# Shared-key attention with split scores: queries and keys in high and low halves, three products in place of one

## The reference, cut to what matters

```python
def dilated_group(q, k, v, slopes, window, dilation):
    ...
    scores = jnp.einsum("bpnqhd,bpnkhd->bpnhqk", qb, kw) * (1.0 / math.sqrt(dh))
    ...
    scores = jnp.where(valid[:, None], scores + bias, NEG_INF)
    m = jnp.max(scores, axis=-1, keepdims=True)
    p = jnp.exp(scores - m)
    denom = jnp.sum(p, axis=-1, keepdims=True)
    ...
def dilated_attention(x, k, v, w_q, w_o):
    q = (x @ w_q).reshape(bsz, s, N_GROUPS, N_HEADS, HEAD_DIM).astype(jnp.float32)
    for g, (window, dilation) in enumerate(DILATION_PAIRS):
        o, l = dilated_group(q[:, :, g], k, v, slopes, window, dilation)
    ...
    return out.reshape(bsz, s, N_HEADS * HEAD_DIM).astype(x.dtype) @ w_o
```

## Time and profile before

| what | value |
|---|---|
| median of 3 runs | 1755.33 us |
| profiled execution | 1756.47 us, its span 1754.7 us |
| PE busy | 1717.1 us, 98% of the span |
| DVE busy | 1243.8 us, 71% |
| ACT busy | 976.3 us, 56% |
| chain that ended last | PE 88%, DVE 7%, ACT 3%, issue 2% |
| scores of this stage, L780 | 1% of the chain |
| granted PE clock, mean | 0.992 |

### The profile page before, as it was taken

The page is one execution under the profiler, slowest core; times in us unless marked ns, Lnnn a source line. Parts: engine busy times, 40 slices in busy tenths (PEclk is TensorE's granted clock), DMA queues, the critical chain, the costliest instruction groups (busy, mean ns, idle before and its releaser), DMA issues.

```text
span 1754.7 us, 33254 instructions
## 1 busy us (share of the span) xinstructions
PE 1717.1 (98%) x11724; PEld 1559.4 (89%) x11724; DVE 1243.8 (71%) x2166; ACT 976.3 (56%) x1710; POOL 49.3 (3%) x33
## 2 busy tenths in 40 slices
PE   9999998999999999999899999999999999999998
PEld 7888898888899888888788888989999999888887
DVE  6776789777664776677787766868656567787765
ACT  5564596655455655466565544565533346665543
POOL 0000100100010000000010001001000010010000
PEclk9999999999999999999999999999999999999999
DMA  6555455455544556433255564333455533345562
GB/s 225 191 200 194 133 181 182 143 185 199 196 140 157 202 185 219 160 118 123 87 208 192 191 201 147 99 119 133 144 171 193 178 126 134 112 141 195 189 201 90
DMA packets 76349, 288.80 MB, mean 165 GB/s; under 512 B 9312, under 2 KB 11616, under 8 KB 76256
## 3 DMA queue, kind: packets, MB, share of 16 engines
q1 hardware_dynamic: 76256, 287.53, 48.6%
HBM read 286.45 MB, written 1.05 MB: 164 GB/s over the span
## 4 chain that ended last, share of the span: by engine, by line
PE 88%; DVE 7%; ACT 3%; issue 2%; DMA 0%; ACTq 0%; SPq 0%; DVEq 0%
PE psum L532 32%; PE psum L533 17%; PE psum L524 11%; PE psum L526 10%; PE psum L525 10%; DVE wlo L1580 1%; ACT whi L1105 1%; PE psum L780 1%; DVE sums L1710 1%; PE psum L610 1%; PE psum L657 1%; PE psum L662 1%; DVE r_sq L1717 1%; DVE sums L1725 1%; PE psum L696 1%
## 5 line engine op out<-in xcount | busy, mean ns | idle before, releaser
L1580 DVE TENSOR_TENSOR wlo<-raw,whi 128x1024 fp32r<-128x1024 f32 (+2 forms) x485 | 630.5, 1307 | 288.2 <-ACT whi L1105 287.4
L532 PE MATMUL psum<-x_split,whi 128*128 128x512 f32 x1760 | 618.3, 395 | 3.1 <-DVE x_split L1615 2.0
L1105 ACT ACTIVATE whi<-raw 128x1024 fp32r<-128x1024 f32 (+2 forms) x494 | 545.5, 1116 | 39.5 <-PE psum L526 20.9
L533 PE MATMUL psum<-x_split,wlo 128*128 128x256 f32 x1760 | 494.3, 281 | 0.0
L532 PEld LDWEIGHTS psum<-x_split,whi 128*128 128x128 f32 x1760 | 331.1, 188 | 80.8 <-DVE x_split L1615 2.3
L524 PE MATMUL psum<-x_split,whi 128*128 128x272 f32 (+1 forms) x1168 | 341.4, 292 | 4.5 <-DVE x_split L1780 4.2
L526 PE MATMUL psum<-x_split,wlo 128*128 128x272 f32 (+1 forms) x1168 | 333.7, 286 | 0.0
L525 PE MATMUL psum<-x_split,whi 128*128 128x272 f32 (+1 forms) x1168 | 332.8, 285 | 0.0
L533 PEld LDWEIGHTS psum<-x_split,wlo 128*128 128x128 f32 x1760 | 331.5, 188 | 0.0
L532 PE MATMUL psum<-h_split,whi 128*128 128x512 f32 x770 | 272.2, 397 | 0.0
L524 PEld LDWEIGHTS psum<-x_split,whi 128*128 128x128 f32 x1168 | 219.9, 188 | 11.4 <-issue 8.6
(11 more groups left out here) (233 smaller groups left out, 1711.0 us busy)
## 6 DMA issues: line engine op xcount, KB each, us to landing
raw<-w_in SPq DMA_DIRECT2D x264, 512.0 KB, 3.2
raw<-w_out SPq DMA_DIRECT2D x96, 704.0 KB, 4.3
raw<-w_mix SPq DMA_DIRECT2D x42, 512.0 KB, 3.3
raw<-w_rg SPq DMA_DIRECT2D x25, 512.0 KB, 3.9
raw<-w_q SPq DMA_DIRECT2D x24, 512.0 KB, 3.3
raw<-w_kv SPq DMA_DIRECT2D x16, 512.0 KB, 3.3
raw<-w_mixo SPq DMA_DIRECT2D x16, 512.0 KB, 3.2
raw<-w_rg_out SPq DMA_DIRECT2D x8, 640.0 KB, 3.9
```

Source lines behind the costliest of these rows:

```text
L532: nc.tensor.matmul(ps[:, bank, :], whi[slot][:, w], split, start=start, stop=False)
L533: return nc.tensor.matmul(part(bank, 0), wlo[slot][:, w], split[:, 0], start=False, stop=stop)
L1105: nc.scalar.activation(whi[slot][:, 0:cols], raw[slot][:, 0:cols], ACT.Copy).then_inc(w_hi_done, count)
L1580: V.tensor_tensor(wlo[slot][:, 0:cols], raw[slot][:, 0:cols], f(whi[slot][:, 0:cols]), ALU.subtract).then_inc(w_lo_done, 1)
```

## The change

Queries and keys are split too. ACT's copy of a query tile out of PSUM now writes `q_hi` in fp32r (24 times, as before); a new instruction of DVE, `rest_of_query(s)`, reads the same bank again, scales it and subtracts `q_hi`, which gives `q_lo`; it, not ACT, now signals `acc_free`. For each of the 8 pairs ACT makes `k_hi` from `kT` (`high_keys`), and DVE `k_lo` (`rest_of_keys`). `scores` issues three fp32r products in place of one float32 product, for each of two query halves and two heads, and waits also for `k_lo_done`. DVE's `rest_of_query(s)` stands at the end of step s, behind `bias_max`, `sum_groups` and `rest_of_output`; the keys of pair hp are split in step max(0, 3 hp - 2).

```diff
--- before.py
+++ after.py
@@ -205,7 +205,7 @@
     cursor[0] = mix_at
     kT = place("kT", [KD, SEQ])
     v_tok = place("v_tok", [2, D])
-    qT = place("qT", [2, GROUPS, SEQ])
+    q_hi = place("q_hi", [2, GROUPS, SEQ], fp32r)
     dist = place("dist", [GROUPS, SCORES])
     s_even = place("s_even", [2, GROUPS, SCORES])
     nmax_g = place("nmax_g", [2, 2, 2, GROUPS])
@@ -219,6 +219,11 @@
     s_odd = place("s_odd", [2, GROUPS, SCORES])
     assert cursor[0] <= hlo_at
     s_pair = (s_even, s_odd)
+    cursor[0] = hlo_at + KD * TOK * 4
+    q_lo = place("q_lo", [2, GROUPS, SEQ], fp32r)
+    k_hi = place("k_hi", [2, SEQ], fp32r)
+    k_lo = place("k_lo", [2, SEQ], fp32r)
+    assert cursor[0] <= hlo_at + KF * TOK * 4
 
     cursor[0] = mix_at
     con2 = place("con2", [N_B])
@@ -344,6 +349,9 @@
     rg_ready = sem("rg_ready")
     vT_done = sem("vT_done")
     v_copied = sem("v_copied")
+    q_hi_done = sem("q_hi_done")
+    k_hi_done = sem("k_hi_done")
+    k_lo_done = sem("k_lo_done")
     round_scored = sem("round_scored")
     round_biased = sem("round_biased")
     scored = sem("scored")
@@ -443,6 +451,7 @@
     token_starts = lambda T: [tok0(T) + min(t * P, T - P) for t in range(-(-T // P))]
 
     two_banks = lambda s: s % 2
+    key_step = lambda hp: max(0, GROUPS * hp - 2)
     round_bank = lambda n, e: 2 + 2 * (n % 2) + e
     mix_evicted = lambda st, kind, n: st.u0 + MIX_SLOT[kind, n] + 1
     decayed = lambda h: s_fox[:, h, 0:KEYS_ALL] if h < 2 else pT_fox[:, h - 2, :]
@@ -770,15 +779,17 @@
                 hp, g = n // GROUPS, n % GROUPS
 
                 pe.wait_ge(acc_free, st.u0 + n + 1)
+                pe.wait_ge(k_lo_done, hp + 1)
                 if n >= 2:
 
                     pe.wait_ge(round_biased, n - 1)
                 for queries, keys in ((slice(0, P), slice(0, P)), (slice(P, SEQ), slice(0, SEQ))):
-                    for e in range(2):
-                        rows = slice(HD * e, HD * (e + 1))
-                        cols = TOKEN_TILES[queries.start // P]
-                        last = nc.tensor.matmul(ps[:, round_bank(n, e), cols], qT[rows, hp % 2, g, queries], kT[rows, hp, keys],
-                                                start=True, stop=True)
+                    for m, (q, k) in enumerate(((q_hi, k_hi), (q_hi, k_lo), (q_lo, k_hi))):
+                        for e in range(2):
+                            rows = slice(HD * e, HD * (e + 1))
+                            cols = TOKEN_TILES[queries.start // P]
+                            last = nc.tensor.matmul(ps[:, round_bank(n, e), cols], q[rows, hp % 2, g, queries], k[rows, hp % 2, keys],
+                                                    start=queries.start == 0 and m == 0, stop=m == 2, skip_group_check=True)
                 last.then_inc(round_scored, 1)
 
             def transposed(a):
@@ -1374,8 +1385,14 @@
                 if hp >= 2:
 
                     act.wait_ge(round_scored, s - 2 * GROUPS + 1)
-                nc.scalar.activation(qT[:, hp % 2, g, :], acc(two_banks(s), SEQ), ACT.Copy,
-                                     scale=par[:, C_QS + hp:C_QS + hp + 1]).then_inc(acc_free, 1)
+                nc.scalar.activation(q_hi[:, hp % 2, g, :], acc(two_banks(s), SEQ), ACT.Copy,
+                                     scale=par[:, C_QS + hp:C_QS + hp + 1]).then_inc(q_hi_done, 1)
+
+            def high_keys(hp):
+                if hp >= 2:
+
+                    act.wait_ge(round_scored, GROUPS * (hp - 1))
+                nc.scalar.activation(k_hi[:, hp % 2, :], kT[:, hp, :], ACT.Copy).then_inc(k_hi_done, 1)
 
             def exps(a):
                 hp, e = a // 2, a % 2
@@ -1401,6 +1418,9 @@
             for s in range(Q_TILES + 7):
                 if s < Q_TILES:
                     round_ahead(st, s // SLOTS, s % SLOTS)
+                for hp in range(PAIRS):
+                    if key_step(hp) == s:
+                        high_keys(hp)
                 if s >= 8 and s % 3 == 2:
                     copy_transposed(2 * ((s - 8) // 3) + 1)
                 if s >= 9 and s % 3 == 0:
@@ -1924,10 +1944,23 @@
                 dve.wait_ge(at_hi, hp + 1)
                 V.tensor_tensor(h_lo[:, hp, 0:SEQ], acc(7, SEQ), f(h_hi[:, hp, 0:SEQ]), ALU.subtract).then_inc(at_ready, 1)
 
+            def rest_of_keys(hp):
+                dve.wait_ge(k_hi_done, hp + 1)
+                V.tensor_tensor(k_lo[:, hp % 2, :], kT[:, hp, :], f(k_hi[:, hp % 2, :]), ALU.subtract).then_inc(k_lo_done, 1)
+
+            def rest_of_query(s):
+                hp, g = s // GROUPS, s % GROUPS
+                dve.wait_ge(q_hi_done, s + 1)
+                V.scalar_tensor_tensor(q_lo[:, hp % 2, g, :], acc(two_banks(s), SEQ), par[:, C_QS + hp:C_QS + hp + 1],
+                                       f(q_hi[:, hp % 2, g, :]), ALU.mult, ALU.subtract).then_inc(acc_free, 1)
+
             dve.wait_ge(bias_landed, 16)
             for s in range(Q_TILES + 7):
                 if s < Q_TILES:
                     rest(s)
+                for hp in range(PAIRS):
+                    if key_step(hp) == s:
+                        rest_of_keys(hp)
                 if 2 <= s < Q_TILES + 2:
                     bias_max(s - 2)
                 if 5 <= s < Q_TILES + 4 and s % 3 == 2:
@@ -1936,6 +1969,8 @@
                     sum_groups(2 * ((s - 6) // 3) + 1)
                 if s >= 9 and s % 3 == 0:
                     rest_of_output((s - 9) // 3)
+                if s < Q_TILES:
+                    rest_of_query(s)
                 if s in (Q_TILES + 3, Q_TILES + 5):
                     rest_of_chunk(*ahead(by_name["o"], 0, (s - Q_TILES) // 2 - 1))
             add_to_ax(by_name["o"])
```

## The result

The changed kernel takes 1760.37 us (median of 7 runs, 1758.18 to 1762.24), the kernel before beside it 1755.74 (7 runs). The ratio is 1.0028, with a 95% interval of 1.0016 to 1.0039: 0.28% slower. It is the first rival's case (1759.0 to 1760.7), not the forecast of 1757.3; the stated range, 1754.0 to 1761.0, held it.

What follows compares the result with a forecast made beforehand. The prediction took PE's string of work to bound the kernel. Start +1.64 and rounds +0.3, all else 0, gave +1.9 us: 1757.3 us from a median of 1755.33, range 1754.0 to 1761.0.

Steps and rivals of the forecast that it cites:

- first rival: PE's longer idle time ahead of the first scores lowers the clock behind it: 1759.0 to 1760.7 us, chance 0.35.
- the forecast of 1757.3: Whole kernel: later start plus slightly longer rounds, clock not falling, +0.11%; chance 0.50.
- What bounds the kernel: Attention stage: a string of PE work; other engines matter only where they open a wait.
- The start, +1.64: Start of the attention stage: first scores wait for DVE's q_lo, 762.36 instead of 760.72, +1.64 us.
- PE's rounds, +0.3: 24 rounds of scores: three fp32r products take 0.872 us a round against 0.86, +0.3 us in all.
- -3.6: PE's rounds if no product is held up by its weight load; the hidden-loads rival, 1753.4 us, chance 0.09.
- -1.9 us: PE's rounds by the Trainium skill's 81 ns for each weight load: 0.782 us a round.
- The steady steps, 0: Later steps of the stage: DVE's and ACT's added work fits in their idle time, costing 0.
- The tail, 0: End of the stage: q_lo(23) is ready in time and the 1.2 us wait hangs on ACT's last exponentials, 0.
- The clock: Behind the wait ahead of the first scores: forecast kept clock 1.00; a fall would cost 1.7 to 3.4 us, chance 0.35.

Runs made afterwards that it cites:

- e4: The changed kernel with the scores put back to one float32 product of q_hi and kT (q_lo made, not used): 1760.91 us against 1755.39 before.
- e6: The kernel before with one added wait, first scores waiting for VectorE's low half of chunk 5: 1761.09 us against 1755.17, ratio 1.0034.
- e8: The changed kernel with its narrow products 256 columns wide in place of 128: 1760.56 us, ratio 1.0029 to the kernel before.
- e1: The changed kernel with 20 extra unused matmuls ahead of the first round of scores: 1758.21 us against 1755.39 for the kernel before.
- e7: The kernel before with the added wait of e6 and 22 extra unused matmuls ahead of it: 1758.77 us against 1755.17, ratio 1.002.

## Why the prediction was wrong in its likeliest case

- **What bounds the kernel**: right. PE is in a string of work from the first scores to the tail, so each microsecond at the start counts in full.
- **The start, +1.64**: right in mechanism and size, 1.68 measured. `q_lo` took 0.48 us, not the 0.42 of L1717. L1717 has no scale per partition (`par`); the nearer row was L1780, whose median is 0.48 us in the trace before:

```profile
L1780 DVE SCALAR_TENSOR_TENSOR x_split<-r_sq,par,x_split x72: 467/480/1197, 202.8 to 1562.6; 128x256 fp32r<-128x256 f32 x48, 128x272 fp32r<-128x272 f32 x24
```

- **PE's rounds, +0.3**: right in mechanism, mis-sized. A round takes 0.888, not 0.872 us: +0.03 a round, 0.74 us, and 0.3 more in the tiles. The narrow products stand 0.11 us apart, as the one-column row had said, so neither -3.6 nor -1.9 us came.
- **The steady steps, 0**: right (e4). **The tail, 0**: right.
- **The clock**: this is the step that failed. I held the forecast without a fall likelier (0.50) than with it (0.35), on the ground that two waits of 2.2 us had left the clock at 1.00. That ground was a single execution. The same two waits stand in every kernel here, and the clock fell behind one of them in 6 of the 13 profiled executions, that of the changed kernel among them. Before, and in the changed kernel:

```profile
281.90:285.30 3.40, 1.23 (x11) 1.03 (x10) 3.06 (x5) 0.84 (x1) 0.00 (x0) 1.00 0.42 158
285.30:288.70 3.40, 2.49 (x22) 2.28 (x21) 2.20 (x5) 1.88 (x3) 0.00 (x0) 1.00 0.00 0
```

```profile
282.20:285.60 3.40, 1.23 (x11) 1.03 (x10) 3.06 (x5) 0.84 (x1) 0.00 (x0) 1.00 0.46 173
285.60:289.00 3.40, 3.40 (x18) 3.40 (x18) 2.27 (x4) 1.76 (x3) 0.00 (x0) 0.50 0.00 0
```

PE did the same ahead of both, and only one fell; so a wait of about 2 us that left the clock alone once was no evidence against a fall behind 2.9. Nor does PE's busy share tell: 1.23 of 3.40 us stands in both rows, and near 1100 us the clock fell behind 3.16 of 3.40:

```profile
1096.40:1099.80 3.40, 3.16 (x29) 3.08 (x29) 2.45 (x5) 1.93 (x7) 0.00 (x0) 0.99 0.00 0
1099.80:1103.20 3.40, 3.40 (x18) 3.40 (x18) 0.37 (x2) 1.21 (x2) 0.00 (x0) 0.50 0.02 7
```

What the runs showed in its place, one profiled execution for each kernel: the clock fell in all four kernels that left 2.9 us or more of the wait ahead of the first scores idle (after, e4, e6, e8), in neither of the two that filled it (e1, e7), and in none of the seven with 1.5 us or less there. Shorter waits elsewhere are open: behind the tail's later wait of 1.6 us, outside the two stretches, it fell in 6 of the 13. The price is 1.5 us, a little under the rival's 1.7 to 3.4; with a longer gap 2.8.

The sum as measured: 1.68 (start) + 1.51 (clock) + 1.05 (products) = 4.2 us, by the stage alone. The forecast left out the 1.5 and had 0.75 too little for the products. The runs say 4.6 (medians) to 4.9 (ratio), the spans of the two profiled executions 3.4: falls of the clock elsewhere differ from execution to execution (near 285 us only after, near 1554 only before).

The Trainium skill's account (TensorE: Matmul & The Clock Gate, section "HAM oscillation — how this bites in real kernels"), that a wait between bursts makes the array start cold again, agrees with e6 (3.5 us idle, clock 0.50) and e7 (filled, 1.00). Its example has waits of about 3 to 5 us. The prediction said that by it a fall behind 2.9 us would be the forecast; that goes further than the example does, and the four runs, not the page, show the fall.

## What to carry to other kernels

When a step adds work between a tile and its first consumer, look where the first instance stands in each engine's queue: work that is free in the steady steps can be the whole loss at the start. Price a wait of TensorE by its length and by the clock behind it, and do not take it from one trace that a wait leaves the clock alone: the same wait may bring it down in the next execution. Splitting a float32 product in three saves a quarter of the streamed time (0.48 against 0.64 us a round) only on paper, while each narrow product still brings a load of its own weights.

## What the runs showed of the hardware

A wait of 2.9 to 3.5 us with TensorE idle brought its clock from 2.4 to 1.2 GHz for 3.4 to 6.8 us, in each of the four profiled executions that had one; 20 to 22 matmuls whose results nobody uses, in the same idle time, kept it at 2.4 GHz and cost nothing that the stretches show (9.20 against 9.22 us, 98.16 against 98.15). Waits of 2.1 and 2.2 us near 280 us brought it down in 6 of 13. fp32r products stream a column in about one cycle with 128 columns too (0.058 us more for 128 more columns, e8), and two of them in the two row halves start within 0.004 us of each other, yet behind weights of 128 columns the next pair comes no closer than 0.11 us. Filling three waits of 1.5 to 2.1 us elsewhere was worth 2.9 us by the medians, 2.3 by the ratio (0.7 to 3.9).
